# Cross attention's sample values taken for four batches at a time, and separate buffers for the output projection's operand, in a decoder step on one Trainium2 core

## What is computed

```python
def cross_attn(h, mk, mv, wq, wo):
    q = (h @ wq).reshape(B, T, CA_HEADS, CA_HD)
    s = jnp.einsum('bthd,bmhd->bhtm', q, mk).astype(jnp.float32) * CA_HD ** -0.5
    p = jax.nn.softmax(s, axis=-1)
    o = jnp.einsum('bhtm,bmhd->bthd', p.astype(mv.dtype), mv).reshape(B, T, CA_HEADS * CA_HD)
    return o @ wo

def swiglu(h, wg, wu, wd):
    return (jax.nn.silu(h @ wg) * (h @ wu)) @ wd
...
x = x + cross_attn(rmsnorm(x, norm_ca), mem_k, mem_v, ca_wq, ca_wo)
x = x + swiglu(rmsnorm(x, norm_ffn), ffn_w_gate, ffn_w_up, ffn_w_down)
```

## Time and profile before

| | |
|---|---|
| median of 3 runs | 1214.78 us (1214.52 to 1218.22) |
| the profiled execution | 1220.85 us, of which the span of its trace is 1219.0 us |
| PE busy | 1162.3 us, 95% of the span |
| DVE, ACT, POOL busy | 563.3, 452.4, 351.2 us |

### The profile page before, as it was taken

How to read it: one execution, slowest core, us unless ns; L and a number is a source line. 1 busy time by engine, 2 the same in 40 slices (tenths; PEclk the granted TensorE clock), 3 DMA queues, 4 the chain that set the end, 5 groups by cost and what they waited for, 6 DMA issues and landing times.

```text
span 1219.0 us, 20689 instructions
## 1 busy us (share of the span) xinstructions
PE 1162.3 (95%) x8995; PEld 1033.6 (85%) x8995; DVE 563.3 (46%) x771; ACT 452.4 (37%) x756; POOL 351.2 (29%) x222
## 2 busy tenths in 40 slices
PE   5998999999899999999899998999999999999998
PEld 4997464456689999779899885989999999999998
DVE  5423144677335664466630442674444544422332
ACT  6324355577443125221442333143333333321111
POOL 0232110210233263134023200434444333334341
PEclk9998899999999999889999999999999999999999
DMA  6443240420705251213672335223232323222221
GB/s 194 127 125 86 87 122 1 138 70 1 251 31 174 70 172 45 69 53 123 222 281 84 137 157 191 70 70 104 71 104 70 104 70 104 72 94 96 76 81 74
DMA packets 91393, 130.13 MB, mean 107 GB/s; under 512 B 6676, under 2 KB 78728, under 8 KB 89000
## 3 DMA queue, kind: packets, MB, share of 16 engines
q1 hardware_dynamic: 83448, 101.71, 25.6%
q0 software_dynamic: 7856, 27.11, 6.6%
HBM read 120.38 MB, written 12.59 MB: 109 GB/s over the span
## 4 chain that ended last, share of the span: by engine, by line
PE 86%; DVE 7%; ACT 4%; issue 2%; DMA 1%; SPq 0%; DVEq 0%; ACTq 0%
PE ring L729 47%; PE hold L815 6%; PE ring L703 5%; PE ring L1209 2%; PE ring L1124 2%; PE ring L1223 2%; PE ring L1408 1%; PE ring L790 1%; PE ring L910 1%; PE ring L1490 1%; PE ring L1357 1%; PE ring L1471 1%; PE ring L921 1%; PE ring L713 1%; DVE weight_lo L622 1%
## 5 line engine op out<-in xcount | busy, mean ns | idle before, releaser
L622 POOL TENSOR_TENSOR weight_lo<-w_ring,weight_hi 128x1024 fp32r<-128x1024 f32 (+1 forms) x108 | 263.5, 2441 | 570.5 <-ACT weight_hi L1646 570.5
L1646 ACT ACTIVATE weight_hi<-w_ring 128x1024 fp32r<-128x1024 f32 (+1 forms) x135 | 140.3, 1040 | 396.0 <-PE ring L729 335.1
L729 PE MATMUL ring<-operand_hi,weight_hi 128*128 128x272 f32 (+1 forms) x1200 | 249.9, 289 | 2.8 <-DVE operand_lo L2845 1.7
L729 PE MATMUL ring<-operand_lo,weight_hi 128*128 128x272 f32 (+1 forms) x1200 | 249.0, 288 | 0.0
L729 PE MATMUL ring<-operand_hi,weight_lo 128*128 128x272 f32 (+1 forms) x1200 | 248.0, 288 | 0.0
L729 PEld LDWEIGHTS ring<-operand_hi,weight_hi 128*128 128x128 f32 (+1 forms) x1200 | 187.8, 188 | 7.1 <-issue 5.9
L729 PEld LDWEIGHTS ring<-operand_lo,weight_hi 128*128 128x128 f32 (+1 forms) x1200 | 187.7, 187 | 0.4
L729 PEld LDWEIGHTS ring<-operand_hi,weight_lo 128*128 128x128 f32 (+1 forms) x1200 | 187.7, 187 | 0.4
L1626 ACT ACTIVATE arena<-ring 128x1024 f32<-128x1024 f32 (+9 forms) x85 | 61.2, 727 | 101.7 <-PE ring L729 57.1
L815 PE MATMUL hold<-arena,w_ring 128*128 128x504 f32 (+1 forms) x192 | 79.6, 536 | 4.2 <-DVE arena L2257 3.0
L2750 DVE TENSOR_TENSOR x_res<-x_res,ring 128x544 f32<-128x544 f32 x24 | 17.3, 720 | 127.5 <-PE ring L729 127.2
(11 more groups left out here) (426 smaller groups left out, 2055.3 us busy)
## 6 DMA issues: line engine op xcount, KB each, us to landing
w_ring<-in_w_in SPq DMA_DIRECT2D x13, 1024.0 KB, 5.5
w_ring<-in_ffn_w_gate SPq DMA_DIRECT2D x11, 1024.0 KB, 5.3
w_ring<-in_ffn_w_up SPq DMA_DIRECT2D x11, 1024.0 KB, 5.3
w_ring<-in_ffn_w_down SPq DMA_DIRECT2D x8, 1024.0 KB, 5.1
arena<-in_cache_mem_k SPq DMA_DIRECT2D x6, 1024.0 KB, 7.5
arena<-in_cache_mem_v SPq DMA_DIRECT2D x5, 1024.0 KB, 10.5
w_ring<-in_ca_wk SPq DMA_DIRECT2D x4, 1024.0 KB, 5.1
w_ring<-in_ca_wv SPq DMA_DIRECT2D x4, 1024.0 KB, 5.3
```

What stands on the lines that cost most here:

```text
L622: self.ops.tensor_tensor(half_of(WL, self.x, kk, cols), w, half_of(WH, self.x, kk, cols).bitcast(F32), ALU.subtract).then_inc(sem("weights ...
L729: last = mm(ps[0:cols, hf * 512:hf * 512 + HALF], half_of((WH, WL)[pw], x, KT, cols)[:, i, :], (xh, xl)[px][:, k, hf * HALF:(hf + 1) * HAL ...
L1646: fn(half_of(WH, y, kk, cols), w, COPY).then_inc(sem("weights_hi"), 1)
```

## The change

Four edits go together.

1. Values: the four even batches are done side by side (one batch after the other within each half and block), then `cross_weigh(3)`, then the four odd batches. `cross_values_used` is now raised after the even batches and after the first half of the odd ones.
2. Batch 5 gets a buffer of its own, `RC[6]`, in the space of the queries; SP issues it with the four loads before it, after a wait for `cS 3` in place of the one for the first pair.
3. The projection's operand is in new buffers `CRH` and `CRL`. DVE instead of ACT copies `hold` to `crow`, in halves; between and behind the halves it makes rows of `CRL`.
4. With `OPH` and `OPL` free during `wo`, ACT and DVE fill them for the FFN row by row as the items of `wo` are done, and the sum over the squares is moved behind row 3 of the first item of `ffg`.

```diff
-          ("v", 0, 2), ("v", 2, 3), ("v", 4, 4), ("v", 6, 5), ("v", 1, 0), ("v", 3, 1), ("v", 5, 2)]
+          ("v", 0, 2), ("v", 2, 3), ("v", 4, 4), ("v", 6, 5), ("v", 1, 0), ("v", 3, 1), ("v", 5, 6)]
+SUM_AT = 4
...
+        RC.append(QC.rearrange("p k t -> p (k t)")[:, DM:DM + 2048].rearrange("p (j n) -> p j n", j=2))
+        CRH, CRL = [rounded(n, base["arena"] + 4 * at, KT * TOK).rearrange("p (k t) -> p k t", k=KT)
+                    for n, at in (("crossed_hi_rows", 4096), ("crossed_lo_rows", ARENA - KT * TOK - 4))]
...
-            cross_weigh(3)
-            evac(pe, ("csPT",))
-            open_hold(("cO",))
-            for pair in ((0, 2), (4, 6), (1, 3), (5, 7)):
-                for b in pair:
+            def sample_values(odd):
+                for b in range(odd, DB, 2):
                     _, s, c = cross_in("v", b)
                     pe.wait_ge(s, c)
                 for hf in range(2):
                     for j in range(2):
-                        for b in pair:
+                        for b in range(odd, DB, 2):
...
+                    if odd == 1:
+                        last.then_inc(sem("cross_values_used") if hf == 0 else hold_full, 1)
+                    elif hf == 1:
+                        last.then_inc(sem("cross_values_used"), 1)
+            evac(pe, ("csPT",))
+            open_hold(("cO",))
+            sample_values(0)
+            cross_weigh(3)
+            sample_values(1)
...
-            norm_sum(2)
+            sums = open_item(("sum", 2))
+            ps = open_item(("ffg", 0))
+            for k in range(KT):
+                if k == SUM_AT:
+                    pe.wait_ge(sem("square_sums"), 2)
+                    pe.wait_ge(sem("squares"), KT * 2)
+                    for r in (0, KT - 1):
+                        for hf in range(2):
+                            last = mm(sums[:, hf * 512:hf * 512 + HALF], ones[:, :],
+                                      SQ[2][:, r, hf * HALF:(hf + 1) * HALF], start=(r == 0), stop=(r == KT - 1))
+                    last.then_inc(psum_full, 1)
+                normed(2)(k)
...
 # ACT
-            act.wait_ge(sem("cross_values_used"), 2)
+            act.wait_ge(sem("cross_values_used"), 1)
             for k in range(KT):
-                fn(OPH[:, k, 0:SEQ], MX[:, k, 0:SEQ], COPY).then_inc(sem("crossed_hi"), 1)
-            act.wait_ge(hold_full, hold[("cO",)] + 1)
-            fn(crow, HOLD[:, :], COPY).then_inc(hold_free, 1)
+                fn(CRH[:, k, 0:SEQ], MX[:, k, 0:SEQ], COPY).then_inc(sem("crossed_hi"), 1)
...
+            for k in range(KT):
+                if k < KT - 1:
+                    split_to(splits[("wo", 0, 0)] + k + 2)
+                evac(act, ("wo", k))
+                fn(OPH[:, k, :], X[:, k, :], COPY, scale=GV[:, V_FFN + k:V_FFN + k + 1]).then_inc(sem("normed_hi"), 1)
             split_to(splits[("ffg", 0, 1)])
-            full(act, ("wo", KT - 1))
-            for k in range(KT):
-                act.wait_ge(sem("squares"), KT + k + 1)
-                fn(OPH[:, k, :], X[:, k, :], COPY, scale=GV[:, V_FFN + k:V_FFN + k + 1]).then_inc(sem("normed_hi"), 1)
...
 # DVE
+            dve.wait_ge(sem("cross_values_used"), 2)
+            step(cp(crow[:, 0:512], HOLD[:, 0:512]))
+            crossed_lo(range(2))
+            dve.wait_ge(hold_full, hold[("cO",)] + 1)
+            cp(crow[:, 512:1024], HOLD[:, 512:1024]).then_inc(hold_free, 1)
+            crossed_lo(range(2, 4))
...
-            residual("wo", 2)
-            dve.sem_inc(sem("dve_phase"), 1)
-            for k in range(KT):
+            crossed_lo(range(4, KT))
+            def gated_lo(k):
                 dve.wait_ge(sem("normed_hi"), KT * 2 + k + 1)
                 stt(OPL[:, k, :], X[:, k, :], GV[:, V_FFN + k:V_FFN + k + 1], OPH[:, k, :].bitcast(F32), ALU.mult,
                     ALU.subtract).then_inc(sem("normed"), 1)
+            residual("wo", 2, gated_lo)
+            gated_lo(KT - 1)
...
 # SP
             full(sp, ("cx", 7, 1))
-            cross(10, 14)
-            sp.wait_ge(sem("cross_values_used"), 1)
-            cross(14, 15)
+            full(sp, ("cS", 3))
+            cross(10, 15)
```

More of the change, by code:

```diff
@@ L524, in build @@
         wkv_in = [sem(f"window_in{k}") for k in range(2 * RAWS)]
-        cload = [sem(f"cross_in{k}") for k in range(6)]
+        cload = [sem(f"cross_in{k}") for k in range(6)] + [sem("mem_in")]
         sload = [sem(f"state_in{k}") for k in range(HH)]
@@ L538, in cross_in @@
             k = CLOADS[x][2]
-            return RC[k], cload[k], 16 * sum(load[2] == k for load in CLOADS[:x + 1])
+            return RC[k], cload[k], 16 * (sum(load[2] == k for load in CLOADS[:x + 1]) + (k == 6))
         def cross_rows(ps, h):
@@ L1546, in crossed @@
             def crossed(k):
-                pe.wait_ge(sem("crossed"), KT + k // 2 + 1)
+                pe.wait_ge(sem("crossed"), KH + k // 2 + 1 if k < KH else CH + k + 1)
             for n in range(4):
-                feature_major("wo", n, crossed if n == 0 else nothing)
-            norm_sum(2)
+                for m in range(2):
+                    ps = open_item(("wo", 2 * n + m))
+                    split_product(("wo", n, m), ps, range(KT), CRH, CRL, crossed if n + m == 0 else nothing,
+                                  True, True).then_inc(psum_full, 1)
+            sums = open_item(("sum", 2))
+            ps = open_item(("ffg", 0))
+            x = splits[("ffg", 0, 0)]
+            pe.wait_ge(sem("weights_lo"), x + 1)
+            for k in range(KT):
[8 more added lines that the diff above has]
+                normed(2)(k)
+                for i, (pw, px) in enumerate(passes):
+                    for hf in range(2):
+                        last = mm(ps[:, hf * 512:hf * 512 + HALF], half_of((WH, WL)[pw], x)[:, k, :],
+                                  (OPH, OPL)[px][:, k, hf * HALF:(hf + 1) * HALF],
+                                  start=(k == 0 and i == 0), stop=(k == KT - 1 and i == 2), skip_group_check=True)
+            last.then_inc(psum_full, 1)
+            split_product(("ffg", 0, 1), open_item(("ffg", 1)), range(KT), OPH, OPL, nothing, True, True).then_inc(
+                psum_full, 1)
             def hidden(k):
@@ L1556, in _ @@
             for n in range(FT // 2):
-                feature_major("ffg", n, normed(2) if n == 0 else nothing)
+                if n:
+                    feature_major("ffg", n)
                 feature_major("ffu", n)
@@ L2741, in memory_lo, with residual @@
                 dve.sem_inc(sem("dve_phase"), 1)
-            def residual(name, n_norm):
+            def residual(name, n_norm, after=None):
                 for m in range(KT):
@@ L2752, in residual @@
                     square(n_norm, m)
+                    if after and m:
+                        after(m - 1)
                     if name == "ffd":
@@ L2827, in _, with crossed_lo @@
             ts(yP, yP, msc[:, 1:2], None, ALU.mult).then_inc(sem("cross_smp"), 1)
-            dve.wait_ge(sem("cross_smp"), 1)
-            for k in range(KT):
-                dve.wait_ge(sem("crossed_hi"), k + 1)
-                tt_(OPL[:, k, 0:SEQ], MX[:, k, 0:SEQ], OPH[:, k, 0:SEQ].bitcast(F32),
-                    ALU.subtract).then_inc(sem("crossed"), 1)
+            dve.wait_ge(sem("mem_v_out"), 16)
+            def crossed_lo(rows):
+                for k in rows:
+                    dve.wait_ge(sem("crossed_hi"), k + 1)
+                    tt_(CRL[:, k, 0:SEQ], MX[:, k, 0:SEQ], CRH[:, k, 0:SEQ].bitcast(F32),
+                        ALU.subtract).then_inc(sem("crossed"), 1)
+            dve.wait_ge(sem("cross_values_used"), 2)
[4 more added lines that the diff above has]
+            crossed_lo(range(2, 4))
             key = ("csO",)
@@ L2835, in _ @@
                 dve.wait_ge(sem("crossed_hi"), KT + h // 2 * 2 + 2)
-                pair = [T_[:, 2 * h:2 * h + 2, SEQ:TOK].rearrange("p k (b t) -> p k b t", b=DB) for T_ in (OPL, OPH)]
+                pair = [T_[:, 2 * h:2 * h + 2, SEQ:TOK].rearrange("p k (b t) -> p k b t", b=DB) for T_ in (CRL, CRH)]
                 ins = tt_(pair[0], cross_rows(slot(key), h), pair[1].bitcast(F32), ALU.subtract)
                 ins.then_inc(sem("crossed"), 1)
-            dve.wait_ge(sem("crossed"), KT + CH)
+            dve.wait_ge(sem("crossed"), KH + CH)
             dve.sem_inc(freed(key), 1)
-            residual("wo", 2)
-            dve.sem_inc(sem("dve_phase"), 1)
-            for k in range(KT):
+            crossed_lo(range(4, KT))
+            def gated_lo(k):
                 dve.wait_ge(sem("normed_hi"), KT * 2 + k + 1)
```

8 lines of the change are left out of this document (4 added, 4 removed).

## The result

In 15 runs each, the changed kernel took 1208.8 us in the median (1199.7 to 1213.48), the kernel before 1217.34 us (1214.52 to 1221.15). The ratio is 0.9928, with a 95% interval of 0.991 to 0.9946: 8.8 us faster (6.6 to 11.0), against 9.3 forecast. As a time, 1205.5 us was forecast (1203.0 to 1209.5); most of the 3.3 us between that and 1208.8 is the starting point, since the 1214.78 us that it was taken from were the median of the first three of these fifteen runs. A second set of 12 runs, beside 17 of the kernel before, gave 0.9928 again (0.9908 to 0.9949).

What follows compares the result with a forecast made beforehand. PE, busy 95% of the span, was taken as the bound. Values 5.1 us plus way into the FFN 4.2 gave 9.3, from the median 1214.78 to 1205.5 us; range 1203.0 to 1209.5.

Steps and rivals of the forecast that it cites:

- Four at once cost no more a round than two: Values on PE: a round for four batches takes 0.43 us, as for two; at most 0.1 a round more.
- PE stands ahead of the even batches for batch 6's load: Before the even batches: batch 6 lands at 735.0, so PE waits about 1.4 us.
- Batch 5 lands in a tie with `cross_weigh(3)`: Before the odd batches: batch 5 lands at 742.4, `cross_weigh(3)` ends at 742.35; an earlier landing gives nothing.
- DVE's two copies: Ahead of the transposes: DVE copies each 512-column half of `hold` in 0.62 us; the two rows cost 0.2 us.
- The values' term: From the last prompt tile to `wo`: `wo` starts at 748.9 in place of 754.05, 5.1 us gained.
- The way into the FFN: From `wo`'s end into `ffg`: 7.85 us in place of 12.0, 4.2 gained, of which 1.35 half clock, 2.4 two waits.
- A `wo` beyond 48.3 us: Projection: a sign of being wrong; `wo` was forecast to stay at 48.2 us.
- DVE has 0.95 us to spare an item: In `wo`'s items: DVE's idle 1.72 us less 0.77 for the new row leaves 0.95.
- The formula for what comes after: DVE in `wo`: with a row of x us, final lateness is 7 (x - 1.72), all but 1.3 us lost.
- the rivals: DVE late in `wo`: behind at its end, 1209.8 us, chance 0.07; weights split late, 1220.2 at 4.0 a row, chance 0.04.
- It comes back in the FFN: Rival, FFN: PE stands later for 1/rms, losing up to 4.2 us; with late batch 5, 1211 to 1214; chance 0.05.

Runs made afterwards that it cites:

- weigh_first: Changed kernel with `cross_weigh(3)` ahead of both groups of batches; 20.6 us from `cross_weigh(2)` to `wo`, against 20.4.
- late_load: Changed kernel with batch 5's load issued only after the even batches; 15.3 us from the even batches' start to `wo`, against 14.2.
- earlier: Changed kernel with batch 4 in the new buffer, ACT copying the samples' probabilities first, one operand row between the halves of `hold`; ratio to the kernel before 0.991.
- sum_first: Changed kernel with the sum over the squares ahead of `ffg`'s first row; 9.75 us from `wo`'s end to `ffg`'s second item, against 7.85.
- rows_more1: Changed kernel with DVE writing each row of the FFN's low operand but the last twice; `wo` 48.2 us, way to `ffg`'s second item 7.85 us.
- rows_more2: Changed kernel with DVE writing each row of the FFN's low operand but the last three times; way to `ffg`'s second item 9.5 us, ratio to kernel before 0.9943.
- values_only: Changed kernel with its fourth edit undone: FFN operand and sum made after `wo` again; ratio to the kernel before 0.9958.
- before_again: The unchanged kernel before, profiled once more; span 1205.7 us, 12.2 us from the sum's start to `ffg`'s second item.

## Why the prediction held

- *Four at once cost no more a round than two.* Right: 0.43 us. It was read from two pairs that overlapped by chance in the trace of before, a few rows that carried 3.5 of the 5.1 us.
- *PE stands ahead of the even batches for batch 6's load.* Right, 1.30 us, 1.4 forecast. The landing was in the profile before, where nobody waited for it; `weigh_first` shows that this wait only replaces the other.
- *Batch 5 lands in a tie with `cross_weigh(3)`.* Right: it lands 13.6 us after `cross_weigh(2)`'s start (740.7 less 727.13), where 742.4 less 728.75, or 13.65, was forecast, and `late_load` puts its price at 1.1 us.
- *DVE's two copies.* Too low by a little: a copy of 512 columns takes 0.69 us, not 0.62, and with the two rows between, the second half was copied 0.35 us after it was there (744.90, against 743.96 + 0.59). The stand ahead of the transposes is 1.18 us, where it was 1.22 with ACT's single copy, so the halves by themselves gained nothing; `earlier`, with one row between, has 0.91. The values' term falls 0.3 us short (20.44 less 20.15): the odd batches start 0.13 us later than forecast, counted from `cross_weigh(2)`, and the rest comes by DVE's copies.
- *The way into the FFN.* Right, 7.85 us, and `sum_first` splits it. But the 12.1 us against which it is set are one of two values, and in that there was luck: the clock fell there in three of four executions, so that the mean of the way before is nearer 11.8, 0.3 us less. And it fell at `wo`'s start in two of eleven profiles of the new order; if that belongs to the change, which is not shown, it takes another 0.3 us (a fifth of 1.45). An estimate of the mean gain from these numbers is 9.0 - 0.6 = 8.4 us, within the measured interval. A `wo` beyond 48.3 us was one of the prediction's own signs of being wrong; it is there in those two profiles (49.6 and 49.7), by the clock alone.
- *DVE has 0.95 us to spare an item.* 0.83, and `rows_more1` uses it up without loss. The formula for what comes after (7 times what a row takes beyond 1.72 us) gave 4.4 us of lateness where 1.8 came, so the price that the rivals took from it was too high at this length of a row.
- *It comes back in the FFN.* In the changed kernel, no: 404.8 us from `ffg`'s second item to the end, as before. But the mechanism exists. ACT's weight blocks stand in its order behind the pieces that want 1/rms; the first of these starts 3.0 us after `ffg`'s second item in the changed kernel, 6.8 us after it in `rows_more2` and 6.4 in `values_only`. In these two PE stood 0.68 us for `weight_lo` at 813.92 and 0.27 at 818.47; in the changed kernel's profiles there is no such stand.

## What to carry to other kernels

An operand buffer that two phases share makes the second phase start from nothing when the first ends; with buffers of their own, the second's rows can be made item by item, and the price is then spare time of the engine that makes them. Count that spare time with the waits that a neighbouring engine causes in it, here 2.1 us an item. When a wait is taken away, look for the transfer or copy that would end next: here it was a load nobody had waited for. And compare stages by their own intervals, since whole spans here differ by more than the change.

## What was not expected of the hardware

- TensorE's granted clock falls to 1.2 GHz behind the same short stands in some executions and not in others: between `wo` and the FFN (stands of 0.65 and 1.73 us) in three of four, at the start of `wo` (stands of 1.2 and 0.8 us before it) in two of eleven. Each time it cost 1.4 to 1.6 us.
- What DVE loses to POOL's instruction depends on how late DVE is: 2.1 us an item on time, 1.5 when it lags. So its backlog nearly stops growing (6.09 us an item against 6.02).
- The same program reached `cross_weigh(2)` at 728.75 us in one execution and 717.56 in another. The traces show where: by 345 us `before_again` is 4.9 us ahead, by 530 us 11.1. From 325 to 350 us PE stands 2.9 us in `before`, at a mean granted clock of 0.93, and 0.8 us at 1.00 in `before_again`; from 485 to 540 us the clock is 0.81 and 0.94. Why the longer stand comes, and why the clock differs, was not looked into.
